# Seven products for pairs of hidden tiles in the last network's first projection, with weight sums prepared in memory

## The reference, cut to what matters

```python
D_MODEL, SEQ, D_FF = 1024, 512, 2816
def swiglu(h, w_in, w_out):
    gate, up = jnp.split(h @ w_in, 2, axis=-1)
    return (jax.nn.silu(gate) * up) @ w_out
def residual_post_norm(x, y, gate, weight, gain, bias):
    return layer_norm(DN_ALPHA * x + weight * gate[:, None, :] * y, gain, bias)
x = residual_post_norm(x, swiglu(modulate(x, m, 2), ffn2_w_in, ffn2_w_out), m[:, 8], 0.5, ln_gain[2], ln_bias[2])
```

## Time and profile before

| | us |
|---|---|
| median of 3 runs | 1334.32 |
| lowest and highest | 1333.84, 1335.79 |
| time of the profiled execution | 1336.66 |
| its span | 1334.8 |

### The profile page before, as it was taken

How to read it: one execution, slowest core, us unless ns; L and a number is a source line. 1 busy time by engine, 2 the same in 40 slices (tenths; PEclk the granted TensorE clock), 3 DMA queues, 4 the chain that set the end, 5 groups by cost and what they waited for, 6 DMA issues and landing times.

```text
span 1334.8 us, 17708 instructions
## 1 busy us (share of the span) xinstructions
PE 1307.2 (98%) x7134; PEld 1102.9 (83%) x7134; DVE 825.3 (62%) x1165; ACT 546.5 (41%) x740; POOL 83.0 (6%) x91
## 2 busy tenths in 40 slices
PE   8999999999999999999999999999999999999996
PEld 5778888888889999888888888887788888888885
DVE  5446688666686777565227678878763223335888
ACT  5525221222212544565325645556552222224553
POOL 1000000000000000000202221220000000000000
PEclk8999999999999999999999999999999999999998
DMA  9965545665545667553432478266435333333562
GB/s 320 275 180 175 186 164 164 185 180 172 178 158 156 177 189 190 174 174 126 138 122 64 83 200 220 54 148 150 142 95 158 95 111 95 96 95 110 190 205 102
DMA packets 217378, 206.74 MB, mean 155 GB/s; under 512 B 7322, under 2 KB 175880, under 8 KB 216592
## 3 DMA queue, kind: packets, MB, share of 16 engines
q1 hardware_dynamic: 202328, 151.39, 38.5%
q0 software_dynamic: 14272, 52.53, 13.9%
q10 hardware_dynamic: 696, 1.68, 0.4%
HBM read 203.46 MB, written 25.18 MB: 171 GB/s over the span
## 4 chain that ended last, share of the span: by engine, by line
PE 84%; DVE 6%; ACT 3%; issue 2%; DMA 2%; SPq 2%; DVEq 0%; ACTq 0%
PE ps L2199 27%; PE ps L2201 26%; PE ps L2200 26%; DMA w_raw<-ffn_w_in 1%; DVE w_lo L1448 1%; DMA gain_bias_b<-w_ada 1%; PE ps L2238 1%; SPq L770 1%; PE ps L2662 1%; PE ps L2647 1%; ACT w_hi L957 1%; PE ps L2251 0%; PE ps L2681 0%; SPq L766 0%; DVE xl L1570 0%
## 5 line engine op out<-in xcount | busy, mean ns | idle before, releaser
L2199 PE MATMUL ps<-h_hi,w_lo 128*128 128x512 f32 (+1 forms) x1120 | 391.5, 350 | 1.9 <-DVE w_lo L1796 1.4
L2201 PE MATMUL ps<-h_hi,w_hi 128*128 128x512 f32 (+1 forms) x1120 | 387.7, 346 | 0.0
L2200 PE MATMUL ps<-h_lo,w_hi 128*128 128x512 f32 (+1 forms) x1120 | 387.7, 346 | 0.0
L1448 DVE TENSOR_TENSOR w_lo<-w_raw,w_hi 128x2048 fp32r<-128x2048 f32 (+1 forms) x116 | 256.3, 2210 | 157.9 <-ACT w_hi L957 157.7
L957 ACT ACTIVATE w_hi<-w_raw 128x2048 fp32r<-128x2048 f32 (+1 forms) x116 | 214.2, 1848 | 274.0 <-PE ps L2201 259.9
L2199 PEld LDWEIGHTS ps<-h_hi,w_lo 128*128 128x128 f32 x1120 | 211.7, 189 | 32.2 <-issue 4.2
L2201 PEld LDWEIGHTS ps<-h_hi,w_hi 128*128 128x128 f32 x1120 | 211.7, 189 | 27.0
L2200 PEld LDWEIGHTS ps<-h_lo,w_hi 128*128 128x128 f32 x1120 | 211.8, 189 | 25.5
L2199 PE MATMUL ps<-w_hi,h_lo 128*128 128x512 f32 x298 | 117.0, 393 | 1.4 <-DVE w_lo L1448 1.4
L1460 DVE SCALAR_TENSOR_TENSOR ada_row<-ada_block,c_cols,ada_row 128x256 f32<-128x256 f32 x224 | 108.6, 485 | 8.0
L2199 PE MATMUL ps<-h_hi,half_lo 128*128 128x512 f32 (+1 forms) x272 | 101.9, 375 | 0.7 <-ACT beside_lo L1286 0.4
(11 more groups left out here) (297 smaller groups left out, 1699.5 us busy)
## 6 DMA issues: line engine op xcount, KB each, us to landing
w_raw<-ffn_w_in SPq DMA_DIRECT2D x124, 512.0 KB, 5.2
ada_block<-w_ada POOLq DMA_DIRECT2D x28, 1024.0 KB, 5.7
w_raw<-ffn_w_out SPq DMA_DIRECT2D x55, 512.0 KB, 4.3
weight_sums<-ffn_w_out POOLq DMA_DIRECT2D x6, 2816.0 KB, 21.6
half_raw<-w_mix_in SPq DMA_DIRECT2D x48, 256.0 KB, 3.4
w_raw<-weight_sums SPq DMA_DIRECT2D x20, 512.0 KB, 4.0
ada_block<-w_ada SPq DMA_DIRECT2D x6, 1024.0 KB, 9.7
weight_sums<-weight_sums POOLq DMA_DIRECT2D x2, 2816.0 KB, 17.9
```

Of the source, the lines that this page charges most:

```text
L1448: nc.vector.tensor_tensor(lo, raw, hi.bitcast(F32), ALU.subtract).then_inc(s_lo[s], 1)
L2199: nc.tensor.matmul(dst, s_low, m_high, start=start, stop=False, skip_group_check=shared)
L2200: nc.tensor.matmul(dst, s_high, m_low, start=False, stop=False, skip_group_check=shared)
L2201: return nc.tensor.matmul(dst, s_high, m_high, start=False, stop=stop, skip_group_check=shared)
```

## The change

It has three parts.

1. **Pairs of hidden tiles.** L2 keeps 4 jobs "in" (`WHOLE`). The other 18 hidden tiles are made in 9 pairs. A pair's product is [256 + 256 tokens] x [512 + 512 rows] x [256 gate + 256 up columns], again by seven block products: each has 4 row blocks, 2 column tiles and 256 tokens, which is 24 matmuls of 256 columns. A pair has four jobs: part 0 with P1 and P5, part 1 with P6 and P3, part 2 with P7 and P2, part 3 with P4. Part 0 loads a quarter of the weights and one of two weight sums kept in memory (`i_sums`). Part 1 loads one quarter and part 2 the other memory sum and a quarter. The weights of P6 and of P4 are added by VectorE in the raw buffer (`add_inner_weights`), and part 3 loads nothing. P1, P5 and P6 are copied out of PSUM, P3, P7 and P2 joined on VectorE. The four sums of input quarters that serve as left operands (`input_sum`) are made at the start of L2, in new buffers `h_sums` and `third_sum`.
2. **The memory sums.** GpSimd issues eight copies of 128 x 2304 elements (1.18 MB each) in L1, between `ada_block` loads, four accumulating transfers of the same size late in L1, and four more in the mixer, after groups 1, 2 (two) and 4.
3. **The second projection** takes P2 before P7. P7 is copied by ScalarE as it ends. The early parts of the outputs of P2 and P7 (the copies of P1 and P5) are scaled and added to the residual some jobs earlier (`add_early`), the late products after them (`add_late`), in place of the joins.

Smaller moves: the gate row's transpose and its spread are made in pairs 1 to 3, the load of the last gain and bias follows part 0 of pair 1, and each of the first six `pair`-made left sums covers one or two tiles.

```diff
-SEVEN = ("P1", "P5", "P6", "P3", "P7", "P2", "P4")
+SEVEN = ("P1", "P5", "P6", "P3", "P2", "P7", "P4")
...
+WHOLE = 4
+PAIRS = (22 - WHOLE) // 2
+PAIR_PARTS = (("P1", "P5"), ("P6", "P3"), ("P7", "P2"), ("P4",))
...
+                jobs.extend((tag, "pair", t, part) for t in range(PAIRS) for part in range(len(PAIR_PARTS)))
...
+        return [(tag, 0, half, i) for half, tiles in ((1, (0, 1)), (0, (0, 1)), (1, (2, 3)), (0, (2, 3))) for i in tiles]
...
+                if key[1:2] == ("pair",):
+                    _, _, t_, part = key
+                    c0 = (WHOLE + 2 * t_) * P
+                    blocks = raw.rearrange("p (b k c) -> p b k c", k=4, c=256)
+                    if part == 0:
+                        sp.wait_ge(s_wadd, 2 * t_)
+                        sp.wait_ge(s_isum, 64)
+                        sources = (w2i[:, 0:4, c0:c0 + 256], i_sums[0][:, :, c0 - WHOLE * P:c0 - WHOLE * P + 256])
+                    elif part == 1:
+                        for k in (0, 2):
+                            sp.dma_start(blocks[:, 1, k:k + 2, :], w2i[:, 4 + k:6 + k, FF + c0:FF + c0 + 256]).then_inc(s_loaded[s], 16)
+                        return
+                    else:
+                        sp.wait_ge(s_wadd, 2 * t_ + 1)
+                        sp.wait_ge(s_isum, 128)
+                        sources = (i_sums[1][:, :, c0 - WHOLE * P:c0 - WHOLE * P + 256], w2i[:, 4:8, c0:c0 + 256])
+                    for b, src in enumerate(sources):
+                        sp.dma_start(blocks[:, b, :, :], src).then_inc(s_loaded[s], 16)
...
+            def copy_inner(which, n):
+                pool.dma_start(inner_rows(which, n), inner_block(0, which, n)).then_inc(s_icopy, 16)
+
+            def add_inner(which, n):
+                pool.dma_start(split_row(inner_rows(which, n)), split_row(inner_block(which, 1, n)), accum_op=ALU.add,
+                               max_dma_last_dim=8192).then_inc(s_isum, 16)
+
             for m in range(ADA_FIRST, ADA_BLOCKS):
                 ada(m)
+                if 11 <= m < 27 and m % 2:
+                    n = (m - 11) // 2
+                    copy_inner(n // 4, n % 4)
+                if m >= 28 and m % 2 == 0:
+                    pool.wait_ge(s_icopy, 128)
+                    add_inner(0, (m - 28) // 2)
...
+                for n in {1: (0,), 2: (1, 2), 4: (3,)}.get(g, ()):
+                    add_inner(1, n)
...
+            def pair_keep(t, p):
+                x = {"P1": halves(glu[:, 0, :]), "P5": hid_last[:, pair_rows(t), 256:512],
+                     "P6": hid_last[:, pair_rows(t), 0:256]}[p]
+                if p == "P5":
+                    wait_done(JOB["L2", "pair", t, 0])
+                else:
+                    act.wait_ge(s_seven, 3 * t + (1 if p == "P1" else 2))
+                if p == "P1":
+                    act.wait_ge(s_hf, pair_hid(t) - (0 if t else 1))
+                nc.scalar.activation(x, halves(ps[:, pair_bank(t, p), :]), ACT.Copy).then_inc(s_kept, 1)
+
+            def pair_silu(t, late):
+                if late:
+                    wait_done(JOB["L2", "pair", t, 3])
+                    act.wait_ge(s_hf, pair_hid(t))
+                    nc.scalar.activation(glu[:, 1, :], ps[:, pair_bank(t, "P4"), :], ACT.Silu).then_inc(s_silu, 1)
+                else:
+                    act.wait_ge(s_joined, 3 * t + 3)
+                    nc.scalar.activation(glu[:, 0, :], glu[:, 0, :], ACT.Silu).then_inc(s_silu, 1)
+
...
+                for t in range(PAIRS):
+                    for part in range(len(PAIR_PARTS)):
+                        pair_split_hi(JOB["L2", "pair", t, part] + 2)
+                        if part == 0:
+                            pair_keep(t, "P1")
+                            pair_keep(t, "P5")
+                        if part == 1:
+                            pair_keep(t, "P6")
+                        if part == 3:
+                            pair_silu(t, 0)
+                            pair_silu(t, 1)
...
+            def add_inner_weights(t, which):
+                first, second, third = (JOB["L2", "pair", t, part] for part in range(3))
+                blocks = [w_raw[s][:, :].rearrange("p (b n) -> p b n", n=1024) for s in (first % 2, second % 2)]
+                if which == 0:
+                    if t:
+                        last = JOB["L2", "pair", t - 1, 3]
+                        dve.wait_ge(s_lo[slot_of(last)], USES[last] + 1)
+                    for i in (first, second):
+                        dve.wait_ge(s_loaded[i % 2], 32 * RAW_LOADS[i])
+                    a, b = blocks[0][:, 1, :], blocks[1][:, 1, :]
+                else:
+                    dve.wait_ge(s_loaded[third % 2], 32 * RAW_LOADS[third])
+                    dve.wait_ge(s_lo[slot_of(second)], USES[second] + 1)
+                    a, b = blocks[1][:, 0, :], blocks[0][:, 1, :]
+                nc.vector.tensor_tensor(blocks[1][:, 0, :], a, b, ALU.add).then_inc(s_wadd, 1)
+
+            def pair_split_lo(i):
+                if i >= SEVEN_FIRST:
+                    split_both_lo(i - SEVEN_FIRST)
+                    return
+                split_lo(i)
+                if JOBS[i][3] == 2:
+                    add_inner_weights(JOBS[i][2], 1)
+
+            def pair_join(t, p):
+                rows, bank = pair_rows(t), halves(ps[:, pair_bank(t, p), :])
+                dve.wait_ge(s_kept, 3 * t + {"P3": 3, "P7": 2, "P2": 1}[p])
+                y = {"P3": hid_last[:, rows, 0:256], "P7": hid_last[:, rows, 256:512], "P2": halves(glu[:, 0, :])}[p]
+                if p == "P7":
+                    dve.wait_ge(s_seven, 3 * t + 3)
+                else:
+                    wait_done(JOB["L2", "pair", t, 1 if p == "P3" else 2])
+                a, b = (bank, y) if p == "P3" else (y, bank)
+                nc.vector.tensor_tensor(y, a, b, ALU.add if p == "P2" else ALU.subtract).then_inc(s_joined, 1)
+
+            def pair_hidden(t, late):
+                dve.wait_ge(s_silu, pair_hid(t) + late + 1)
+                dve.wait_ge(s_joined, 3 * t + 3)
+                x = hid_last[:, pair_rows(t), 256 * late:256 * late + 256]
+                nc.vector.tensor_tensor(x, x, halves(glu[:, late, :]), ALU.mult).then_inc(s_hf, 1)
+
...
+                input_sum_low(3)
+                for t in range(PAIRS):
+                    for part in range(len(PAIR_PARTS)):
+                        pair_split_lo(JOB["L2", "pair", t, part] + 2)
+                        if part == 1:
+                            pair_join(t, "P3")
+                        if part == 2:
+                            pair_join(t, "P7")
+                            if t + 1 < PAIRS:
+                                add_inner_weights(t + 1, 0)
+                            pair_join(t, "P2")
+                    pair_hidden(t, 0)
+                    pair_hidden(t, 1)
+                    first_left_sums(t)
...
+                    if s == 0 and n and before == "P2":
+                        add_late(before, 1)
+                    if s == 0 and n and before == "P7":
+                        add_late(before, 0)
+                        add_late(before, 1)
+                    if n in (4, 5):
+                        add_early("P2", n - 4)
+                    if n in (7, 8):
+                        add_early("P7", n - 7)
...
+            def pair_products(t, part):
+                i = JOB["L2", "pair", t, part]
+                ready(i)
+                w_high, w_low = (x.rearrange("p (b k c) -> p b k c", k=4, c=256) for x in weights(i)[1:])
+                for b, p in enumerate(PAIR_PARTS[part]):
+                    high, low = pair_left(p)
+                    if p == "P1":
+                        pe.wait_ge(s_hf, max(pair_hid(t) - 2, HID["L2", 0, 1] + 1))
+                    if p == "P2" and t == 0:
+                        pe.wait_ge(s_hf, HID["L2", 0, WHOLE - 1] + 1)
+                    if p in ("P5", "P6", "P7", "P3") and t == 0:
+                        pe.wait_ge(s_leftlo, ("P5", "P6", "P7", "P3").index(p) + 1)
+                    if p in ("P6", "P3", "P7"):
+                        pe.wait_ge(s_kept, 3 * t + ("P6", "P3", "P7").index(p) + 1)
+                    if p == "P4":
+                        pe.wait_ge(s_joined, 3 * t + 2)
+                    for u in range(2):
+                        c = slice(u * P, (u + 1) * P)
+                        for k in range(4):
+                            ins = product(ps[:, pair_bank(t, p), 256 * u:256 * u + 256], w_high[:, b, k, c], w_low[:, b, k, c],
+                                          high[:, k, :], low[:, k, :], p in ("P1", "P5", "P2") and u == k == 0, k == 3, True)
+                    if p == PAIR_PARTS[part][-1]:
+                        ins.then_inc(s_done[slot_of(i)], 1)
+                    else:
+                        ins.then_inc(s_seven, 1)
```

(29 more changed lines are left out.)

220 lines of the change are left out of this document (153 added, 67 removed).

## The result

The changed kernel takes 1355.25 us (median of 4 runs, 1352.3 to 1358.35), the kernel before in the same runs 1334.34. The ratio is 1.0155, with a 95% interval of 1.0128 to 1.0182: slower by 20.9 us. The forecast was 1342 and its range ended at 1353. The sign was right and the size was not, and most of the time was lost in another place than the forecast put it. The profiled execution took 1358.35 us with a span of 1356.5, 21.7 more than before.

What follows compares the result with a forecast made beforehand. TensorE, busy throughout both rebuilt stages, was taken as the bound. Pairs +7.0, end -0.8 and memory sums +1.5 gave +7.7 us: 1336.66 to 1344.4 profiled, median 1334.3 to 1342, range 1327 to 1353.

Steps and rivals of the forecast that it cites:

- the memory sums: L1 and mixer: added transfers cost nothing in L1 (at most 2 us), +1.5 us in the mixer (0 to 5).
- a way to be wrong: Whole kernel: the forecast also fails if TensorE's clock falls in the idle times; no size given.
- the mixer pays: Rival, mixer and L1: accumulations delay mixer loads by 5 us or more, L1's by 2; 1348 to 1351, chance 0.12.
- The pairs: L2's first projection: nine pairs replace 18 jobs and take 203.4 us against 196.4, +7.0 us.
- The chain: Pairs: two loads, two splits, two sums and a join through two raw buffers; landings plus 11.4 us, 22.8 a round.
- Part 2's landing: Pairs: time from issue to landing of part 2's load, taken as 5.25 us (4.85 to 5.7).
- Part 0's: Pairs: landing of part 0's load, taken as 6.15 us (5.25 to 7.0), 0.9 of it for part 1's load behind.
- the landings are short: Rival, pairs: average landing 5.0 us, stage 192 us (-4.4), time 1330.6; chance 0.17.
- 16 landings and 112 us: Pairs: stage takes 16 times the average landing plus 112 us, breaking even at a landing of 5.3 us.
- TensorE stays the bound: Rival, pairs: loads arrive in time, -14.5 - 0.8 + 1.5, time 1320.5; chance 0.05.
- The start of L2: Last network's start: input sums, some 7.3 us on VectorE, fit into its 7.72 us idle and cost nothing.
- the end: Second projection's end: VectorE's last chain 1.1 us shorter, ScalarE's copy 0.5 against it; -0.8 us (-1.1 to -0.5).

Runs made afterwards that it cites:

- the third buffer: Changed kernel with the gain and bias rows' 8 KB as raw buffer for each pair's part 2: 1337.01 us; with all eight accumulating transfers moved too: 1319.48 us.
- the moved transfers: Changed kernel with all eight accumulating transfers issued in quiet stretches: 1338.02 us; with only the mixer's four issued earlier: 1338.71 us.
- the plain copies' trace: Changed kernel with the mixer's four transfers at their old places as plain copies instead of accumulating ones: 1347.74 us.

## Why the prediction was right in part and wrong in its size

**The step that failed: the memory sums, +1.5 us with bounds 0 and 5.** Alone they cost 16.9 us in the median (1352.32 against 1335.42); in the profiled execution of the changed kernel it was 20.1, 16.4 of it in the mixer. Three things were wrong in it.

- It priced only the fourth transfer of the mixer, by its bytes (7.4 us of traffic beside the one at 907.64), and capped the loss below that. The wait near 929 did grow, from 1.38 to 6.82 us, as that part of the prediction said it would, so even this one place passed the bound of the whole term.
- It looked at what stood behind the issue in program order and not at what was in flight. The first of the four went out 1 to 2 us behind two transfers of 2.8 MB, beside which the half pieces already took up to 18 us to land; ScalarE waited 4.66 us for one of them. There the new transfer cost 8.7 us with the two behind it. The trace of before held both facts, the landings and the wait, and the prediction cited neither.
- It took a stall at its own length. After 6 us without work TensorE ran at half clock for some 6 us, which added 2.7 us each time. The prediction named this only as a way to be wrong.

The rival "the mixer pays" had this mechanism, with a chance of 0.12, and its 1348 to 1351 was still too low, since it put 5 us or more into the mixer and the mixer took 16. In L1 the prediction looked at the loads "made two jobs ahead"; the loss there (3.7 us in this trace, 0.4 to 1.6 in others) came through the `ada_block` loads on GpSimd's queue, which it did not look at.

**The pairs, +7.0 us: right in mechanism and sign, measured +4.2.** The chain is the one that was laid out, and its fixed links sum to 11.4 us as forecast. Part 2's landing was 5.24 (forecast 5.25). Part 0's was 4.98 (forecast 6.15): the load of part 1 issued right behind it does not slow it (4.55 to 4.76 us for the second piece in eight pairs). So the earlier trace rows was read wrongly: the lateness of those two pieces was taken for the price of a follower, and a follower costs nothing here. Why they were late stays open; no transfer of another queue shows beside the first of them. Seven rounds of 21.7 would be 151.9; they took 157.2 (1059.74 to 1216.97). Of the 5.3 us, 2.7 lie in the round of the gate row's spread, 512 KB which ScalarE's queue sends while part 2's second piece is on its way (forecast 0.6):

```profile
w_raw<-ffn_w_in SPq DMA_DIRECT2D x1, 512.0 KB, 7.4
```

With that piece, issued at 1126.42, the round is 24.4 us. The other long rounds are the first (22.8, second piece 5.8 us) and the last (22.7, 5.55); no transfer of another queue shows beside these two, and their cause stays open. So the term that was mis-sized is the landing. The prediction's terms come to 5.7 us on average over the sixteen, the trace has 5.44. Undisturbed, it was near 5.1, as the rival "the landings are short" had it, and three disturbed rounds kept the stage from its 192 us. The prediction's own sum, 16 landings and 112 us, holds to within 3 us: with the mean landing of each trace it gives 199.1 us here and 202.2, 198.2, 199.5 and 200.5 in four experiments with the same pairs, whose stages took 200.6 and 202.9, 198.7, 200.6 and 203.2.

**TensorE stays the bound.** As a rival for this kernel it was wrong, as expected. But its sum, -14.5 in the pairs and -0.8 at the end, is what the third buffer brought: the stage goes from 196.4 to 181.9 us, which is -14.5, and 1319.48 lies 1 us below the 1320.5 of that rival, whose +1.5 for the sums has gone with their place.

**The start of L2, nothing, and the end, -0.8:** both as forecast, the latter also alone.

The Trainium skill's rule in "DMA: Bandwidth & Descriptors" (Queues, rings and completion order), that an engine takes the descriptors of a ring in order, which the prediction set aside, fits the traces after: a piece with 1.5 MB issued behind it on the same queue (part 0 of pair 1, with gain, bias and part 1 following) landed in 4.6 us, and one with a transfer from another queue beside it took 7.4 us (5.4 to 7.8 in four experiments with the same layout). The 5.9 us of the first piece in the earlier trace rows, which had only its own queue's transfers behind it, is not explained by it. The other figure taken from that page, the estimate of 4.4 us for 1 MB, was rightly set aside: these loads took 5.24 and 4.98 us.

## What to carry to other kernels

Before a transfer is added where "the queues have room", list what is in flight at the moment of issue and which load is already waited for; placed 100 to 170 us earlier, the same bytes cost nothing here, and where they were they cost 16 us. Count fewer matmuls as a gain only when the chain that feeds them fits into the shorter round: two loads, two splits, two sums and a join, one behind the other through two buffers, made 21.7 us against 20.2 of products, and one more buffer turned the change from a loss of 21 us into a gain of 15 together with the moved transfers. An addition or join on the engine that closes such a loop belongs behind the one that releases the next load.

## What the runs showed of the hardware

- A busy share of the 16 DMA engines does not tell what they move. In the changed kernel they are 80% busy and more from 800 to 810 us, with the 2.8 MB accumulation issued at 797.37 in flight, and move 70 to 250 GB/s. From 817 on, when that accumulation is near its end (818.65), the same busy share moves 336 to 438 for 5.6 us. The accumulation issued at 799.25 had not landed then either (836.49), so which of the transfers made the difference is not shown. The slices of 800 to 810, then of 815 to 830:

```profile
DMA  8988999999989999999999999999999999999999
GB/s 74 98 115 131 164 213 197 229 164 180 172 147 180 141 170 201 162 184 219 217 199 199 248 188 201 215 227 197 199 248 188 209 215 219 197 205 244 211 203 217
...
DMA  9999999999999999999998989999898999799999
GB/s 206 212 212 213 221 343 336 351 412 426 397 404 416 396 419 438 384 390 421 378 265 228 280 261 355 358 380 276 221 253 173 205 199 176 161 216 193 199 205 206
```

- An accumulating transfer of 1.18 MB took 8.9 to 11.1 us in the quiet stretches, 12.4 to 14.0 beside the loads of L1, and 37.2 behind two larger ones.
- TensorE idle for 6 us came back at half its full clock, for 5.5 and 6.2 us. Idle times in the pairs were 0.15 to 2.5 us; behind the longest the granted clock was 0.50 for 3.4 us (1136.7 to 1140.1), behind the others it stayed at 1.00. A longer one, 3.1 us before 834.84 in the plain copies' trace, left it at 1.00. So the length of one idle time did not decide it.
